# A 1-core two-block transformer in split fp32: spectra of a conv column group moved ahead of the next group's norms, a low split moved behind the turned rows, identity products during a norm, and the experts' order signalled before the rest of the routing arithmetic

## The reference

```python
# moe_swiglu: 8 experts, 2 per token
logits = hf @ w_router
top_val, top_idx = lax.top_k(logits, 2)
gates = jax.nn.softmax(top_val)
y_e = (silu(x_e @ w_gate[e]) * (x_e @ w_up[e])) @ w_down[e]      # 1024 -> 3584 -> 1024
out = sum of gates * y_e
# conformer_conv
u = hn @ w_pw1 + b_pw1                     # 1024 -> 2048
a, g = jnp.split(u, 2, axis=-1)
u = a * jax.nn.sigmoid(g)
u = causal depthwise conv of u, 31 taps, + b_dw
u = jax.nn.silu(layernorm(u, ln_g, ln_b))
h = h + u @ w_pw2 + b_pw2                  # 1024 -> 1024
```

## Time and profile before

| what | us |
|---|---|
| three runs | 2273.22, 2273.64, 2286.73 |
| median | 2273.64 |
| the profiled execution | 2281.22 |
| its span, first to last instruction | 2279.4 |
| TensorE busy | 2151.9 |
| VectorE busy | 1705.0 |
| ScalarE busy | 1415.2 |
| GpSimd busy | 122.7 |
| the first expert's end (TensorE stands) | 635 to 649 |
| heavy experts | to 1022 |
| light experts | 1022 to 1608 |
| conv stage | 1619 to 1735 |

### The profile page before, as it was taken

One profiled execution on the slowest core, in us unless ns is written; L12 is line 12 of the kernel. 1 busy time (PEld: TensorE's weight loads), 2 busy tenths in 40 slices (PEclk: granted clock), 3 DMA queues, 4 the chain that ended last, 5 costly groups with the idle time before them and its releaser, 6 DMA issues.

```text
span 2279.4 us, 27684 instructions
## 1 busy us (share of the span) xinstructions
PE 2151.9 (94%) x10280; PEld 1736.0 (76%) x10280; DVE 1705.0 (75%) x1580; ACT 1415.2 (62%) x1461; POOL 122.7 (5%) x128
## 2 busy tenths in 40 slices
PE   8999999989979999999888888888989999999998
PEld 7887887877868888887666666666768888888887
DVE  5676545767868888889898989898766557676556
ACT  5644444566757777778787877787535446664445
POOL 0000000005900000000000000001001000000000
PEclk9999999999989999999999999999989999999999
DMA  9307645728989999999999999999633556424642
GB/s 324 97 3 239 203 164 193 248 74 328 360 324 397 386 379 388 369 386 380 387 394 382 395 383 395 380 396 392 221 120 130 186 202 210 159 84 148 228 176 77
DMA packets 275672, 609.03 MB, mean 267 GB/s; under 512 B 10662, under 2 KB 47778, under 8 KB 274914
## 3 DMA queue, kind: packets, MB, share of 16 engines
q1 hardware_dynamic: 271794, 594.43, 71.6%
q0 software_dynamic: 3728, 13.01, 1.6%
q10 hardware_dynamic: 32, 0.02, 0.0%
HBM read 593.24 MB, written 14.16 MB: 266 GB/s over the span
## 4 chain that ended last, share of the span: by engine, by line
PE 65%; DMA 16%; DVE 8%; POOL 4%; ACT 4%; issue 3%; SPq 0%; DVEq 0%; ACTq 0%; POOLq 0%
DMA raw<-in_moe_w_up 13%; PE up L2610 6%; PE up L2611 6%; PE up L2616 6%; DVE wl L2080 5%; PE acc L3450 5%; PE up L3080 4%; PE up L3084 4%; PE up L3087 4%; DMA raw<-in_moe_w_gate 3%; PE acc L3455 3%; PE tp L3417 2%; PE up L3417 2%; ACT wh L1278 2%; PE acc L3168 2%
## 5 line engine op out<-in xcount | busy, mean ns | idle before, releaser
L2080 DVE TENSOR_TENSOR wl<-raw,wh 128x2048 fp32r<-128x2048 f32 x378 | 859.7, 2289 | 120.0 <-ACT wh L1278 119.1
L1278 ACT ACTIVATE wh<-raw 128x2048 fp32r<-128x2048 f32 x378 | 724.8, 1921 | 208.1 <-DMA raw<-in_moe_w_gate 51.7
L1751 DVE TENSOR_TENSOR wl<-raw,wh 128x2048 fp32r<-128x2048 f32 x168 | 384.4, 2291 | 270.9 <-ACT wh L1015 269.9
L1015 ACT ACTIVATE wh<-raw 128x2048 fp32r<-128x2048 f32 x168 | 321.9, 1917 | 279.9 <-PE up L2616 103.5
L2610 PE MATMUL up<-wh,xT 128*128 128x512 f32 x608 | 240.9, 397 | 1.6 <-ACT half L1056 0.8
L2611 PE MATMUL up<-wh,xT 128*128 128x512 f32 x608 | 236.3, 389 | 0.0
L3099 PE MATMUL up<-wl,xT 128*128 128x512 f32 x560 | 159.2, 406 | 30.1 <-DVE wl L2080 28.2
L2616 PE MATMUL up<-wl,xT 128*128 128x512 f32 x608 | 161.9, 388 | 0.0
L3099 PEld LDWEIGHTS up<-wl,xT 128*128 128x128 f32 x560 | 99.7, 188 | 77.3 <-DVE wl L2080 59.0
L3096 PE MATMUL up<-wh,xT 128*128 128x512 f32 x560 | 154.9, 398 | 1.2 <-ACT wh L1278 0.6
L3080 PE MATMUL up<-wh,xT 128*128 128x512 f32 x448 | 123.7, 398 | 14.2 <-ACT wh L1278 14.2
(11 more groups left out here) (508 smaller groups left out, 3359.4 us busy)
## 6 DMA issues: line engine op xcount, KB each, us to landing
raw<-in_moe_w_gate SPq DMA_DIRECT2D x126, 1024.0 KB, 13.0
raw<-in_moe_w_up SPq DMA_DIRECT2D x126, 1024.0 KB, 13.9
raw<-in_moe_w_down SPq DMA_DIRECT2D x126, 1024.0 KB, 12.3
raw<-in_ffn_w SPq DMA_DIRECT2D x64, 1024.0 KB, 5.4
raw<-in_hg_w_in SPq DMA_DIRECT2D x15, 1024.0 KB, 14.0
raw<-in_da_w_in SPq DMA_DIRECT2D x12, 1024.0 KB, 6.3
raw<-in_ffn_w_gate SPq DMA_DIRECT2D x22, 512.0 KB, 6.0
raw<-in_ffn_w_up SPq DMA_DIRECT2D x22, 512.0 KB, 7.6
```

Source lines behind the costliest of these rows:

```text
L1015: f(wh[:, q % SPLITS, :], raw_half(q), ACT.Copy).then_inc(s_hi, 1)
L1278: f(wh[:, x % SPLITS, :], raw[:, x % RAW, :], ACT.Copy).then_inc(moe["hi"], 1)
L1751: V.tensor_tensor(wl[:, q % SPLITS, :], raw_half(q), wh[:, q % SPLITS, :].bitcast(F32), ALU.subtract).then_inc(s_lo, 1)
L2080: V.tensor_tensor(wl[:, x % SPLITS, :], raw[:, x % RAW, :], wh[:, x % SPLITS, :].bitcast(F32), ALU.subtract).then_inc(moe["lo"], 1)
```

## The change

GpSimd signals s_rd twice: once right behind the line that writes the order (new), once at the end as before. VectorE and TensorE wait for the count of 2, SP and ScalarE go on waiting for 1.

In the conv stage VectorE computes the spectra of both steps of a group at once, ahead of the norm of the next group's first step: 0 and 1 ahead of norm 2, 2 and 3 ahead of norm 4, 4 and 5 ahead of norm 6; 6 and 7 stay where they were. The call `split()` behind step 6 is gone, and the one behind the turned rows is `split(3)` instead of `split(2)`: halves 0 to 9 are split in the same order among the norms, half 10 together with 11 and 12. At step 1 the first of its two splits stays (the removed and the kept lines are mixed in the diff; `if s == 1: split()` remains).

ScalarE makes the high part of half 10 behind the gate of step 7, no longer between the gates of 6 and 7.

TensorE runs 20 products of the identity with itself, 128 columns each, into a bank that is free, between the last `from_waves` and the turning of the normed rows.

```diff
--- before.py
+++ after.py
@@ -927,6 +927,7 @@
             link(nc.gpsimd.tensor_scalar(order_f[:, NE:PLACES], order_f[:, NE:PLACES], NE - 1.0, None, ALU.min))
             link(nc.gpsimd.tensor_copy(order_f[:, PLACES:PLACES + 1], rank[:, NE - 1:NE]))
             link(nc.gpsimd.tensor_copy(order_i[:, :], order_f[:, :]))
+            pool.sem_inc(s_rd, 1)
 
             for c in range(2):
                 link(nc.gpsimd.tensor_tensor(wk_place, gate[:, :, 0:NE], rt[:, 1 + c], ALU.mult))
@@ -1463,10 +1464,7 @@
                 if c == 0:
                     for n in range(2):
                         keep_taps(b, n)
-                if (c, b) == (3, 0):
-                    split()
-            if c < 3:
-                split()
+            split()
         warm_up(ACT.Sqrt)
         layer_norms(bias=RMS_BIAS)
         for x, (b, q) in enumerate(COLUMNS):
@@ -2234,7 +2232,7 @@
         light_expert(counter(0, HEAVY), counter(0, HEAVY - 1), "light", heavy_before=True)
         with dve.Fori(0, LAST - HEAVY - 1) as i:
             light_expert(counter(i, HEAVY + 1), counter(i, HEAVY), "light")
-        dve.wait_ge(s_rd, 1)
+        dve.wait_ge(s_rd, 2)
         n_extra = dve.value_load(order_i[0:1, PLACES:PLACES + 1], min_val=0, max_val=MAX_EXTRA)
         with dve.If(n_extra > 0):
             with dve.Fori(0, n_extra) as j:
@@ -2283,6 +2281,8 @@
             g, c, b = g_cv + s, s // NB, s % NB
             if b == 0 and s > 0:
                 split()
+                for n in range(s - 2, s):
+                    spectrum(n)
             dve.wait_ge(s_up, g + 1)
             hf = half[:, g % 2, :]
             link(V.scalar_tensor_tensor(hf.rearrange("p (m n) -> p m n", m=2), up[:, g % 2, :].rearrange("p (m n) -> p m n", m=2),
@@ -2295,10 +2295,6 @@
                 dve.wait_ge(s_T, t_cv[s - 2] + 1)
             V.tensor_tensor(stage[:, g % 2, 0:HALF], hf[:, 0:HALF], hf[:, HALF:W], ALU.mult).then_inc(s_st, 1)
             if s == 1:
-                split()
-            if s >= 2:
-                spectrum(s - 2)
-            if s == 6:
                 split()
             if b == NB - 1:
                 if c < 3:
@@ -2321,7 +2317,7 @@
                                  ALU.subtract, ALU.mult))
             dve.sem_inc(s_norm, 1)
         to_channels(T_cn, None, stage, COLUMNS)
-        split(2)
+        split(3)
         nrows[0] += 16
         dve.wait_ge(s_rows, nrows[0])
         for b in range(NB):
@@ -3225,7 +3221,7 @@
         with pe.Fori(0, HEAVY - 2) as i:
             expert(counter(i, 1), counter(i, 0), "heavy")
         expert(counter(0, HEAVY - 1), counter(0, HEAVY - 2), "light")
-        pe.wait_ge(s_rd, 1)
+        pe.wait_ge(s_rd, 2)
         light_expert(counter(0, HEAVY), counter(0, HEAVY - 1), "light")
         with pe.Fori(0, LAST - HEAVY - 1) as i:
             light_expert(counter(i, HEAVY + 1), counter(i, HEAVY), "light")
@@ -3309,6 +3305,7 @@
         project(g_cv, t_cv, 4, T_cv, 2, enter_cv, bank_read=lambda g: pe.wait_ge(cv_n, g - 1 - g_cv), step=to_waves)
         for n in (6, 7):
             from_waves(n)
+        keep_busy(up[:, 0, :], 20)
         for x, (b, q) in enumerate(COLUMNS):
             normed(N_CB)(b)
             turn_place(T_cn, ctm, x, COLUMNS)
```

## The result

| | before | after |
|---|---|---|
| median, us | 2282.66 (8 runs, 2273.22 to 2288.7) | 2262.98 (8 runs, 2257.96 to 2266.64) |
| profiled execution | 2281.22 | 2262.72 |
| its span | 2279.4 | 2260.9 |
| its mean granted clock | 0.987 | 0.993 |

The ratio is 0.992, 95% interval 0.9902 to 0.9938. The kernel is 19.7 us faster by the medians and 18.5 by the spans, against the 23.9 forecast: 0.8%, so within 1%. The time lies 5.0 us above the upper end of the range. More than that is the base: the three runs at hand had a median of 2273.64, the eight of the result 2282.66.

What follows compares the result with a forecast made beforehand. TensorE, busy 94% of the span, was taken as the bound, so gains come from its standing or lower clock: 16.6 (first expert) + 7.3 (conv stage) = 23.9 us off 2273.64, giving 2249.7; range 2246 to 2258.

Steps and rivals of the forecast that it cites:

- The base: Whole kernel: the sum was taken off the median of the runs shown, 2273.64 us, not the profiled 2281.22.
- The early signal: End of first expert: SP's 19.1 us wait goes; TensorE gets back 14.23 us standing and 2.4 of low clock, 16.6.
- I take the 2.9 us as hidden: Second expert: 1.1 MB moved ahead of the weights, 2.9 us at 382 GB/s, costs nothing given over 6 us reserve.
- rival (b): Second expert: the 1.1 MB ahead of the weights are not hidden, 2.9 us back, 2252.6; chance 0.10.
- The new wait ahead of step 4: Conv stage: spectra 0 and 1 ahead of norm 2 make TensorE wait 1.8 us before step 4.
- The end of the stage: Conv tail: the 2.88 us wait goes, norm 7 isn't behind the split, full clock; statistics start 6.7 us earlier.
- Rival (a): Conv tail: the clock falls in the narrow products, the conv stage gives nothing, 16.6 in all, 2257.0; chance 0.18.
- The identity products: Before the turns: 20 products take 2.4 us inside TensorE's wait for the norm, costing nothing at full clock.
- The late split: Behind the turned rows: half 10 split with 11 and 12, hidden under the output product; 2.3 us without that cover.
- (c): From 612 on: DMA is the bound, so the gain is 19.1 + 7.3, 2247.2; chance 0.05.
- (d): First expert: SP stands at a wait behind s_rd or the queue gives nothing; only the conv stage gains, 2266.3; chance 0.04.
- (e): Conv stage: clock falls in the wait at 1650.2 and stays low to group 3's end, +31 us, about 2290; chance 0.02.

Runs made afterwards that it cites:

- signal: Kernel before with the early signal alone; 2267.1 us against 2278.47, ratio 0.9934 to 0.997.
- conv: Changed kernel without the early signal, so the conv edits alone; 2273.0 us against 2278.47 for the kernel before, ratio 0.9965 to 0.9994.
- taps: Changed kernel with the 31 rows of conv taps loaded in two transfers (16 and 15 rows); 2259.06 us against 2279.28 for the kernel before.
- before_taps: Kernel before with only the conv taps loaded in two transfers instead of one; 2273.8 us against 2279.28.
- mid: Changed kernel with the first s_rd signal given some 10 us later, at 619.6; 2261.45 us, one run, against 2272.29 for the kernel before.
- busy9: Changed kernel with 9 identity products instead of 20; 2262.38 us against 2278.47 for the kernel before.
- busy0: Changed kernel with none of the 20 identity products; 2260.12 us, one run, against 2272.29 for the kernel before.
- spec0: Changed kernel with spectra 0 and 1 back behind steps 2 and 3; 2258.47 us, one run, against 2279.28 for the kernel before.
- best2: Changed kernel with taps in two transfers, 9 identity products, spectra 0 and 1 behind steps 2 and 3; 2255.79 us against 2279.28 for the kernel before.
- split6: Changed kernel with half 10's split back behind step 6, on VectorE and ScalarE; 2266.36 us, one run, against 2272.29 for the kernel before.
- best: Changed kernel with 9 identity products, spectra 0 and 1 behind steps 2 and 3, tables loaded in the fourth heavy expert; 2256.72 us against 2278.47 before.
- late_taps: As best, with the late load of the taps in two transfers; 2258.73 us against 2281.63 for the kernel before.

## Why the prediction was wrong in size and right in kind

- **The base.** The forecast stood on the median of three runs, 2273.64, and set aside the profiled execution, 2281.22, as 0.3% above it. Eight runs had 2282.66. This is 9.0 of the 13.3 us between forecast and result. The three runs reached from 2273.22 to 2286.73, 13.5 us, more than the 12 of the whole range I gave; with the sum on the profiled execution it would have been 2257.3. That uncertainty of the base was in none of the bounds. So the step that put the result outside the range is "the forecast for the median is 2273.64 - 23.9": from 2282.66 the same sum gives 2258.8, and a range as wide around it holds the 2262.98.
- **The early signal, 16.6 us: measured 14.7.** The mechanism is shown by signal and conv. The step of the sum that failed is "I take the 2.9 us as hidden": rival (b), held at 0.10, is what happened, at 1.9 us, with another cause than its own. I reckoned the 1.1 MB by their amount. The earlier trace rows showed the tables without a landing time and I passed over that; taps and before_taps show that a transfer of 124 KB in 31 rows held back the halves behind it by 4.4 to 6.8 us. "8.2 us from issue to landing" was the latency of another stage: right behind the tables it was 19 us.
- **What the 14.23 us were made of.** I gave them to SP's wait whole. 6.5 of them go when the taps go out in two transfers (before_taps); the 7.73 left stand beside 8.4 us without any transfer. A wait of SP of 7.3 us, with transfers in flight throughout, cost 0.5 us of standing (mid).
- **The new wait ahead of step 4: forecast 1.8 us, measured 1.90.** Worked out from norm 2 and step 4's start alone. What I left out is that the clock may fall behind it, for 3.4 us and 1.7 us of price, as in conv, busy9 and busy0. Moving spectra 0 and 1 is the part of the change that costs; spec0 and best2 are the better order.
- **The end of the stage: the statistics 6.7 us sooner, measured 6.0.** Counted from the first `to_waves`, they start at 51.2 us, 50.4 was forecast. Missing are 0.5 us in the waves of 6 and 7, which take 8.8 us and not 5.4 + 2.9, and 0.3 in group 3 and the pause. That norm 7 no longer stands behind the split is shown by split6. That the 2.88 us of the earlier trace rows don't arise is seen in the kernel after; which share the spectra have in it, no run tests alone.
- **Rival (a), at 0.18, fell**: products of 32 and 81 rows on end kept the clock at 1.00 in the kernel after. What the earlier trace rows show at 1626.8, a fully busy stretch followed by 0.50, didn't repeat in the tail. It did repeat at its own place, the taps' waves, in eight of the fourteen traces, the kernel after among them (its stretches stand below this list). The Trainium skill (TensorE: Matmul & The Clock Gate, Part 1: The HAM clock gate) says that the clock follows how busy the engine has been; by that rule the tail would keep it, and it did. The fall at the taps' waves stays unexplained, and so does why the other six traces, with the same code there, don't have it.
- **The identity products: forecast 2.4 us, measured 4.5.** The earlier trace rows count 18 records, which I took for 18 of the 20 calls; a call of fp32 data leaves two records. So they held the turns 0.9 us; the turns themselves took 0.60 each, as forecast. That 0.9 had no effect on the time that can be told: with fewer of them or none the clock falls at the turns.
- **The late split: forecast nothing, measured nothing.** What it brings is split6's 2.4 us (one run).
- **Rivals (c), (d), (e).** (c) fell: TensorE is busy 270.00 of 270 us from 740 to 1010. (d) fell with signal. (e) began in three runs and ended after 3.4 us each time.

The taps' waves in the kernel after, columns as in the earlier trace rows:

```profile
1612.40:1615.30 2.90, 2.90 (x8) 1.06 (x8) 2.09 (x8) 2.84 (x9) 0.84 (x2) 1.00 0.58 185
1615.30:1622.10 6.80, 6.80 (x15) 4.37 (x14) 3.77 (x6) 6.74 (x11) 0.00 (x0) 0.50 0.24 79
```

In all, the sum was 5.4 us too large on the spans (23.9 against 18.5): 1.9 at the second expert, 1.6 at the end of the conv stage, and +1.9, +1.6 and -1.7 in stretches where no code differs in kind.

## What to carry to other kernels

Before a load is called hidden, look at its form, not only at its bytes: one of 31 rows held back the loads behind it at both places where it was issued here, and as 16 and 15 rows it didn't, while the bandwidth hardly differed (366 and 370 GB/s behind it); the time from issue to landing of what comes behind is what shows it. What comes out at the bounding engine of a queue's wait was here not a share of it but what exceeded a reserve, the transfers in flight; the stretch without any is what cost. And where the runs at hand spread as wide as the effect, put the base's own spread into the range.

## What the hardware showed unexpectedly

A DMA queue at 366 GB/s, share 1.04, with no load of 1 MB landing for 9.8 us (rows fetched in by 626.5, next half at 636.3); with the taps in two transfers the same distance is 4.5 us (627.0 to 631.5), at 370 GB/s. And short stretches at 0.50: 71 of the 77 between the start and the end of these fourteen profiled executions last 3.4 or 6.8 us and cost up to half of it. In the conv stage they came 2.9 to 4.1 us behind the start of the taps' waves, with TensorE busy up to them (eight traces); behind a wait of 2.18 us (conv) or 2.19 (busy9, busy0); and behind two waits close together at the turns, of 1.44 and 1.03 us (busy9, best, best2, late_taps) or 3.45 and 1.03 (busy0); but not behind 1.90 or 1.91 (after, taps, mid, split6) nor 2.17 (split6). In best2 the stretches (columns as in the earlier trace rows) show one such step, at the turns, with TensorE standing 2.47 us in the first of them and busy throughout the second:

```profile
1672.00:1679.90 7.90, 5.43 (x35) 4.70 (x35) 5.48 (x10) 2.92 (x7) 0.00 (x0) 1.00 0.11 46
1680.00:1683.30 3.30, 3.30 (x15) 3.11 (x15) 0.87 (x2) 3.24 (x9) 0.64 (x1) 0.50 0.00 0
1683.50:1690.00 6.50, 6.50 (x30) 5.33 (x30) 3.77 (x4) 5.04 (x10) 6.33 (x4) 1.00 0.01 3
```

By these stretches the same code takes 14.61, 16.2 or 17.8 us from the taps' waves to the first `to_waves`, with none, 3.4 or 6.8 us of low clock in it, and single stretches under 2 us can't be given to one edit.
